# Decoder step on one core: the convolution's group norm moved between the third pair's values, its four reciprocals made one, output scales folded into the splits, the last cached values in two more slots

## The reference

```python
x = post(x, 0.5 * swiglu_1(mod(x, 0)), 0)
q, k, v, glu = project(mod(x, 1), w_in)
attn = moba(q, k, v)             # samples: 2048 cached keys/values each, 8 heads of 64
y = depthwise_conv(glu) + b_dw   # 31 taps, 512 channels
g = y.reshape(..., 8, 64)        # 8 groups of 64 channels
g = (g - mean(g)) * rsqrt(mean((g - mean(g)) ** 2) + 1e-5)
conv = silu(g.reshape(y.shape) * gn_g + gn_b)
m = concat([attn * beta_attn, conv * beta_conv]) @ w_out
x = post(x, m, 1)
x = post(x, 0.5 * swiglu_2(mod(x, 2)), 2)
```

## Time and profile before

| what | value |
|---|---|
| median of 3 runs | 952.88 us (950.6 to 952.88) |
| profiled execution: its time | 953.04 us |
| its span, first to last instruction | 951.2 us |
| mean granted TensorE clock | 0.957 |
| TensorE busy | 865.2 us, 91% |
| VectorE, ScalarE, GpSimd busy | 51%, 36%, 28% |

### The profile page before, as it was taken

One profiled execution on the slowest core, in us unless ns is written; L12 is line 12 of the kernel. 1 busy time (PEld: TensorE's weight loads), 2 busy tenths in 40 slices (PEclk: granted clock), 3 DMA queues, 4 the chain that ended last, 5 costly groups with the idle time before them and its releaser, 6 DMA issues.

```text
span 951.2 us, 16893 instructions
## 1 busy us (share of the span) xinstructions
PE 865.2 (91%) x6704; PEld 759.1 (80%) x6704; DVE 481.5 (51%) x764; ACT 342.7 (36%) x466; POOL 266.0 (28%) x319
## 2 busy tenths in 40 slices
PE   6699999997899988999987889867989999999997
PEld 3499989996799968988664556437879999999995
DVE  1543433431333387753686776564774434444436
ACT  2323332331222254455442324253463333342223
POOL 2020000000010014999999999300320000000000
PEclk9599999999899998999999989888999999999999
DMA  9958777777577434334897999994415454644401
GB/s 301 347 184 262 232 221 258 246 233 259 190 236 231 144 110 133 128 94 162 264 359 264 350 359 370 348 348 137 133 46 177 140 166 137 183 143 145 133 1 56
DMA packets 181521, 195.78 MB, mean 206 GB/s; under 512 B 11811, under 2 KB 163609, under 8 KB 181445
## 3 DMA queue, kind: packets, MB, share of 16 engines
q1 hardware_dynamic: 174541, 188.38, 61.3%
q10 hardware_dynamic: 6624, 6.33, 2.1%
q0 software_dynamic: 288, 0.14, 0.1%
HBM read 192.01 MB, written 3.17 MB: 205 GB/s over the span
## 4 chain that ended last, share of the span: by engine, by line
PE 76%; DVE 13%; DMA 4%; ACT 3%; issue 2%; SPq 1%; ACTq 0%; DVEq 0%
PE bank L1389 19%; PE bank L1390 18%; PE bank L1391 18%; PE bank L1605 5%; PE bank L1365 3%; PE bank L1630 3%; DVE wlo L956 2%; DVE kT L1194 2%; PE bank L1402 1%; PE bank L1700 1%; PE bank L1403 1%; PE bank L1404 1%; PE bank L1354 1%; DMA xrow<-in_x_sample 1%; DMA raw<-in_ffn_wg 1%
## 5 line engine op out<-in xcount | busy, mean ns | idle before, releaser
L956 DVE TENSOR_TENSOR wlo<-raw,whi 128x2048 fp32r<-128x2048 f32 (+1 forms) x80 | 190.8, 2386 | 264.1 <-ACT whi L649 264.1
L1389 PE MATMUL bank<-mh,whi 128*128 128x320 f32 x824 | 262.1, 318 | 4.5 <-DVE wlo L956 4.5
L1390 PE MATMUL bank<-ml,whi 128*128 128x320 f32 x824 | 256.5, 311 | 0.0
L1391 PE MATMUL bank<-mh,wlo 128*128 128x320 f32 x824 | 256.4, 311 | 0.0
L649 ACT CAST whi<-raw 128x2048 fp32r<-128x2048 f32 (+1 forms) x80 | 148.6, 1863 | 258.3 <-PE bank L1391 171.3
L1389 PEld LDWEIGHTS bank<-mh,whi 128*128 128x128 f32 x824 | 156.8, 190 | 15.3 <-issue 10.3
L1390 PEld LDWEIGHTS bank<-ml,whi 128*128 128x128 f32 x824 | 156.9, 190 | 0.0
L1391 PEld LDWEIGHTS bank<-mh,wlo 128*128 128x128 f32 x824 | 156.6, 190 | 0.0
L1389 PE MATMUL bank<-hh,whi 128*128 128x320 f32 x352 | 109.7, 312 | 0.0
L1390 PE MATMUL bank<-hl,whi 128*128 128x320 f32 x352 | 108.6, 309 | 0.0
L1391 PE MATMUL bank<-hh,wlo 128*128 128x320 f32 x352 | 108.6, 308 | 0.0
(11 more groups left out here) (233 smaller groups left out, 1161.2 us busy)
## 6 DMA issues: line engine op xcount, KB each, us to landing
araw<-in_w_ada SPq DMA_DIRECT2D x28, 1024.0 KB, 5.1
raw<-in_ffn_wg SPq DMA_DIRECT2D x22, 1024.0 KB, 7.5
raw<-in_ffn_wu SPq DMA_DIRECT2D x22, 1024.0 KB, 6.9
raw<-in_cache_v SPq DMA_DIRECT2D x68, 256.0 KB, 6.1
raw<-in_ffn_wd SPq DMA_DIRECT2D x16, 1024.0 KB, 6.5
raw<-in_cache_k SPq DMA_DIRECT2D x64, 256.0 KB, 4.2
raw<-in_w_in SPq DMA_DIRECT2D x10, 1024.0 KB, 5.4
raw<-in_w_ada SPq DMA_DIRECT2D x8, 1024.0 KB, 12.3
```

The source lines that it names most:

```text
L956: dve.tensor_tensor(wl(slot_w(phase, u))[:, 0:size], landed(phase, u)[:, 0:size], wh(slot_w(phase, u))[:, 0:size].bitcast(F32), ALU.subtra ...
L1389: pe.matmul(bank[:, b, 0:T], wh(slot)[:, c], h_, start=(start and n == 0), stop=False)
L1390: pe.matmul(bank[:, b, 0:T], wh(slot)[:, c], l_, start=False, stop=False)
L1391: ins = pe.matmul(bank[:, b, 0:T], wl(slot)[:, c], h_, start=False, stop=(stop and n == len(parts) - 1))
```

## The change

- `group_means` is hooked after step 3 of `pair_values(2)`, the subtractions stand between two steps of the pair 3 softmax, the squares after its exponentials, and `group_variances` between `pair_values(2)` and `pair_probs(3)`.
- The variances of the 8 groups are taken with a 128 x 32 matrix into 32 partitions for each chunk, all in bank 0. So one root and one reciprocal of 128 x 320 stand for four of each, and `group_scales`, after step 2 of `pair_values(3)`, spreads the result back to 128 partitions by four matmuls over 32 rows.
- ScalarE writes `mh` as value times output scale, and VectorE writes `ml` as value times scale less `mh`. The separate scaling falls away.
- `hi(WOUT, 0)` comes before the Silu, `hi(WOUT, 1)` after the convolution's splits; `lo(WOUT, 0)` before the convolution's `ml`, `lo(WOUT, 1)` after.
- The last eight value chunks go to slots 0, 1, 2, 3, 6, 7, 2, 3. Chunks 60 and 61 lie in `kvw` and no longer wait for steps 0 and 1 of pair 3; `lo` of `WOUT` 0 and 1 wait until they are consumed.
- `conv_half(1)` is cut in two, with `attn_turn(3)` between the halves.
- The constants grow by 160 columns, and `acc` lies in an old tile.

```diff
 def kv_slot(kvi):
-    return kvi % (KV_RING if kvi < KVN - 8 else RING)
+    return kvi % KV_RING if kvi < KVN - 8 else (0, 1, 2, 3, 6, 7, 2, 3)[kvi - KVN + 8]
...
             for u in range(2, WOUT[2]):
-                load(WOUT, u, cols(i["w_out"], slice(UC * u, UC * u + UC)), NCH * UC, (v_used, 24 + 3 + u))
+                load(WOUT, u, cols(i["w_out"], slice(UC * u, UC * u + UC)), NCH * UC, (v_used, 24 + u - 1))
...
+            def group_squares():
+                act.wait_ge(stored_conv, 16 * DB)
+                for c in range(NCC):
+                    act.wait_ge(gc_ready, c + 1)
+                    act.activation(tmp[:, c, :], yT[:, NCC + c, :], ACT.Square).then_inc(gq_ready, 1)
...
                 probs(j)
+                if j == 3:
+                    group_squares()
                 acc_out(j - 1)
...
+            act.wait_ge(gv_mm, 1)
+            act.activation(tmp[:, 0, :], bank[:, 0, 0:T], ACT.Sqrt, bias=con[:, C_EPS:C_EPS + 1]).then_inc(gs_ready, 1)
+            hi(WOUT, 0)
+            act.wait_ge(ge_mm, NCC)
             for c in range(NCC):
                 act.wait_ge(gx_ready, c + 1)
                 act.activation(tmp[:, c, :], yT[:, NCC + c, :], ACT.Silu, scale=par2[:, 4 + c:5 + c], bias=par2[:, 8 + c:9 + c]).then_inc(gy_ready, 1)
+                act.wait_ge(gy_ready, c + 1)
+                act.mul(mh[:, NCC + c, :], tmp[:, c, :], par2[:, 16 + c:17 + c]).then_inc(mh_ready, 1)
+            hi(WOUT, 1)
+            acc_out(3)
+            attn_out(3)
+            act.wait_ge(av_evac, 4)
+            act.wait_ge(pv_out, 4)
+            for c in range(NHP):
+                act.mul(mh[:, c, :], yT[:, c, :], par2[:, 12 + c:13 + c]).then_inc(mh_ready, 1)
...
                 if phase is WOUT and u < 2:
-                    dve.wait_ge(v_used, 24)
+                    dve.wait_ge(v_used, 24 + 5 + u)
...
                 bias_ready(j)
+                if j == 3:
+                    for c in range(NCC):
+                        dve.wait_ge(gm_mm, c + 1)
+                        y = yT[:, NCC + c, :]
+                        dve.tensor_tensor(y, y, bank[:, c, 0:T], ALU.subtract).then_inc(gc_ready, 1)
                 sums_ready(j)
...
+            dve.wait_ge(gs_ready, 1)
+            dve.reciprocal(tmp[:, 1, :], tmp[:, 0, :]).then_inc(gr_ready, 1)
             for c in range(NCC):
+                dve.wait_ge(ge_mm, c + 1)
                 y = yT[:, NCC + c, :]
+                dve.tensor_tensor(y, y, bank[:, c, 0:T], ALU.mult).then_inc(gx_ready, 1)
+            def low_mix(n, src, at):
+                c = MIX_ORDER[n]
+                dve.wait_ge(mh_ready, 16 + n + 1)
+                dve.scalar_tensor_tensor(ml[:, c, :], src, par2[:, at:at + 1], mh[:, c, :].bitcast(F32), ALU.mult, ALU.subtract).then_inc(ml_ready, 1)
+            lo(WOUT, 0)
             for c in range(NCC):
+                low_mix(c, tmp[:, c, :], 16 + c)
             lo(WOUT, 1)
             for c in range(NHP):
+                low_mix(NCC + c, yT[:, c, :], 12 + c)
...
+                steps = {0: lambda: gate_sum(j), 2: lambda: max_swap(j), 5: lambda: prob_sum(j)}
+                if j == 3:
+                    steps[3] = group_means
+                pair_values(j - 1, steps)
+                if j == 3:
+                    group_variances()
                 pair_probs(j)
                 attn_turn(j - 1)
...
             def group_variances():
                 for c in range(NCC):
                     pe.wait_ge(gq_ready, c + 1)
-                    pe.matmul(bank[:, c, 0:T], gnones, tmp[:, c, :], start=True, stop=True).then_inc(gv_mm, 1)
+                    ins = pe.matmul(bank[QG * c:QG * c + QG, 0, 0:T], con[:, C_GSUM:C_GSUM + QG], tmp[:, c, :], start=True, stop=True)
+                ins.then_inc(gv_mm, 1)
+
+            def group_scales():
+                pe.wait_ge(gr_ready, 1)
+                for c in range(NCC):
+                    pe.matmul(bank[:, c, 0:T], con[QG * c:QG * c + QG, C_GOUT:C_GOUT + P], tmp[QG * c:QG * c + QG, 1, :],
+                              start=True, stop=True).then_inc(ge_mm, 1)
...
-            pair_values(3, {0: group_means, 2: group_variances, 6: lambda: conv_half(0)})
-            conv_half(1)
+            pair_values(3, {2: group_scales, 6: lambda: conv_half(0, 0, NCC)})
+            conv_half(1, 0, 2)
             attn_turn(3)
+            conv_half(1, 2, NCC)
```

More of the change, by code:

```diff
@@ L66 @@
 C_TURN = C_SWAP + P
-C_N = C_TURN + P
+C_GSUM = C_TURN + P
+C_GOUT = C_GSUM + QG
+C_N = C_GOUT + P
 def constants():
@@ L104, in constants @@
             c[:, at:at + QG] = ((h[:, None] == 2 * (col[None, :QG] // 8) + e) & (r[:, None] == r_) & (t[:, None] == col[None, :QG] % 8))
+    c[:, C_GSUM:C_GSUM + 2] = (p[:, None] // 64 == np.arange(2)[None, :]) / 64.0
+    c[:, C_GOUT:C_GOUT + P] = p[:, None] % QG == col[None, :] // 64
     return c
@@ L282, in build @@
             qo = sb("qo", [P, DB, NHP, QG], F32, scope)
-            acc = sb("acc", [P, 2, 2 * P], F32, scope)
             vtok = sb("vtok", [P, 2, AW], F32, scope)
@@ L301, in build @@
             pr = sb("pr", [P, 3, 2], F32, scope)
+        acc = ps_[:, 0:2, 0:2 * P]
         s_two = (s_even[:, 0:PAST + 2 * NS].rearrange("p (b c) -> p b c", b=2), s_odd[:, :, :])
@@ L1738, in next_pair @@
                     pe.wait_ge(pt_evac, 5 * j)
-                pair_values(j - 1, {0: lambda: gate_sum(j), 2: lambda: max_swap(j), 5: lambda: prob_sum(j)})
+                steps = {0: lambda: gate_sum(j), 2: lambda: max_swap(j), 5: lambda: prob_sum(j)}
[4 more added lines that the diff above has]
+                    group_variances()
                 pair_probs(j)
                 attn_turn(j - 1)
-            for j in range(1, 4):
-                next_pair(j)
-            pe.wait_ge(pt_evac, 20)
             def group_means():
@@ L1758, in group_variances, with conv_half @@
                     pe.wait_ge(gq_ready, c + 1)
-                    pe.matmul(bank[:, c, 0:T], gnones, tmp[:, c, :], start=True, stop=True).then_inc(gv_mm, 1)
+                    ins = pe.matmul(bank[QG * c:QG * c + QG, 0, 0:T], con[:, C_GSUM:C_GSUM + QG], tmp[:, c, :], start=True, stop=True)
[5 more added lines that the diff above has]
+                              start=True, stop=True).then_inc(ge_mm, 1)
+            for j in range(1, 4):
+                next_pair(j)
+            pe.wait_ge(pt_evac, 20)
             first = [(2 * u + cc, slot_w(WOUT, u), cc, (n_ready, w_used)[cc]) for u in range(2) for cc in range(2)]
-            def conv_half(u):
+            def conv_half(u, c0, c1):
                 pe.wait_ge(w_lo, WOUT[0] + u + 1)
-                products(first[2 * u:2 * u + 2], m_parts(MIX_ORDER[:NCC]), lambda n: pe.wait_ge(ml_ready, 16 + n + 1), stop=False)
-            pair_values(3, {0: group_means, 2: group_variances, 6: lambda: conv_half(0)})
-            conv_half(1)
+                products(first[2 * u:2 * u + 2], m_parts(MIX_ORDER[c0:c1]), lambda n: pe.wait_ge(ml_ready, 16 + c0 + n + 1),
+                         start=c0 == 0, stop=False)
+            pair_values(3, {2: group_scales, 6: lambda: conv_half(0, 0, NCC)})
+            conv_half(1, 0, 2)
             attn_turn(3)
+            conv_half(1, 2, NCC)
             products(first, m_parts(MIX_ORDER[NCC:]), lambda n: pe.wait_ge(ml_ready, 16 + NCC + n + 1), start=False)
```

22 lines of the change are left out of this document (2 added, 20 removed).

## The result

The changed kernel took 941.95 us (median of 4, 938.21 to 943.44), the kernel before 951.74 us (median of 4). The ratio is 0.9892, with a 95% interval of 0.9867 to 0.9917: some 10.3 us faster, 7.9 to 12.7. With more rounds it came out at 0.9905 (0.9884 to 0.9927), 9.0 us. The forecast was a gain of 8.9 us and a time of 944.1, between 941.5 and 947.8. The gain was about right.

What follows compares the result with a forecast made beforehand. The norm's chain was taken to hold `conv_half(0)` through `wlo`, with DMA data as second limit. Gains of 5.7, 1.4 and 1.8, in all 8.9 us, from 953.04 gave 944.1, range 941.5 to 947.8.

Steps and rivals of the forecast that it cites:

- What bounded the kernel: Before `conv_half(0)`: 5.65 us idle for `wlo`, held by the norm's chain; behind it, DMA data set value step 6.
- The front part: Norm work moved to pair 2: means 2.35 us, variances 0.3 us; pair 3's values start at 623.75 instead of 621.1.
- The middle: From the root to the last `ml` in pair 3: `conv_half(0)` has its operands 3.0 us before step 6 ends.
- rival of a late chain by table loads: Silu and `mul` share no table, seven more loads cost 9.0 us, gain 5.6; chance 0.12, at 946.5 to 950.
- Transfers: Loads of the last value chunks: chunks 60 to 62 land when they did; the slots' change counts 0.
- The end: From `conv_half(0)` to the attention's first matmul: gains of 5.7, 1.4 and 1.8 us, in all 8.9.
- the three terms: `conv_half(0)` starts 5.7 us earlier, runs 1.4 shorter, and step 7 to the attention's first matmul takes 1.8 less.
- Against the profiled execution's 953.04 ... 944.1: Whole kernel: the gain of 8.9 us set against the one profiled execution of 953.04 gives 944.1.
- step 6 cannot start before 637.8: Pair 3's value step 6: its start is set by DMA data, a chunk every 3.0 us, whatever the norm does.
- the likeliest case: Whole kernel: time of 944.1, chance 0.80, own range 941.5 to 946.5.

Runs made afterwards that it cites:

- again: The kernel before, unchanged, run against itself and profiled a second time: ratio 0.9985 (0.9968 to 1.0001).

## Why the prediction was right, and where it was off

**What bounded the kernel.** Right. The wait for `wlo` before `conv_half(0)` was the chain of the norm, and behind it stood the data of the last values. The run with a megabyte less shows the second limit, the run with six more reciprocals brings the first one back.

**The front part.** Right that it costs nothing that counts, with its sizes off. The subtractions and the squares fitted in the idle times named. From step 3 of pair 2 to pair 3's values it took 12.43 us (606.69 to 619.12; 12.44 in the second profile), before 11.71 at a clock partly down (0.81 from 606 to 624) and 11.03 in the second profile at the full one. So the moved work costs 0.7 or, both at the full clock, 1.4 us, and the forecast had 2.65. That pair 3's values started at 619.12, not 623.75, has another reason for the larger part: step 3 of pair 2 had already started 2.7 us earlier (606.69 for 609.38), ahead of the change. The page "TensorEngine Tiling (Array Packing)" of the Trainium skill, in "Tiling Modes", has four tiles for matrices of 32 rows as for 32 columns, working side by side; the trace agrees. `group_scales` took 0.82 us, against 2.42 for four full-width matmuls of the same 320 columns, and the forecast had taken the upper bound of 2.35.

**The middle.** Right that it arrives in time: 3.0 us of reserve forecast, 1.9 found, since step 4 ran in part at half clock (1.70 us) and `wlo` waited for it, and since the four `ml` then took 1.93 us, for 1.5. The scaled writes on ScalarE were not the pace: the last ended at 631.64, for 636.1. That is because `group_scales` was done at 623.9, for 630.2, and `WOUT` 0 had landed by 623.77, for 625.7. The rival of a late chain by table loads did not come: two loads, and Silu alternates with the scaled write without one. The further drain that the Trainium skill counts in "ScalarE: Activation LUTs", "What ACT_TABLE_LOAD costs", does not show here: the load ends at 620.32 and the root starts at 620.33, and the same holds at 626.97 and 626.99. Nor does it show ahead of the load, which starts 0.02 us after the work before it ends (619.02 and 625.67). So 1.28 us is the price in this place.

**Transfers.** Right, as far as the runs can tell: with the slots undone the time stays within its interval, and chunk 60 is used when it was although it was issued 0.8 us later.

**The end.** In the first pair of profiles the three terms came out as 5.7, 1.6 and 1.7 for 5.7, 1.4 and 1.8. Only the third is confirmed by more than one pair. The first two fit so well by luck, since forecast and check both used the one execution whose norm came late. Over three profiles with the old norm (before, again, and with the cut alone) step 6 to `conv_half(0)` took 7.58, 6.08 and 6.14 us and `conv_half(0)` 6.49, 5.69 and 5.93. Over five with the new one it was 1.87 each, within 0.01, and 4.91, 4.88, 5.67, 4.78 and 4.95. By the means the terms are 4.7, 1.0 and 1.7, in all 7.4 and not 8.9. What lies between 7.4 and the 9.0 measured (6.9 to 11.0) is not located. In the first changed profile the clock rose after 2.6 us of `conv_half(0)`, 4.4 after the start of step 6; the forecast had 5.2.

**The step that failed** is the last one, "Against the profiled execution's 953.04 ... 944.1", with the range built on it. It takes one execution for the base, and it puts the stretch up to step 6 at nothing, by "step 6 cannot start before 637.8". That holds for that one execution. Step 6 started at 637.80, 637.16, 635.50 and 639.84 in the four profiles with the norm at its old place, and at 635.78, 636.51, 636.61, 637.38, 635.26 and 636.74 in six with it at the new place and the whole stream (634.49 in a seventh, with the idle matmuls). What these follow is the moment at which SyncE comes to chunk 56, between 601.3 and 606.5 and before the change acts; the 33.0 to 33.9 us from there are the same in both kernels. So the 2.0 us by which the changed profile was ahead of the sum are scatter: 1.5 of them lie before the change, and 0.5 are less than the width of those distances. What makes SyncE come to chunk 56 early or late stays open.

The profile used was in two respects a slow one: its time was 1.3 us above the median that the kernel before then showed, 951.74, and it came late to pair 3, in part by a stretch at half clock, so that the wait before `conv_half(0)` was 5.65 and not 4.14 as in the second profile. With 8.9 taken from 951.74 the forecast would have been 942.8. The median of three shown beforehand, 952.88, would not have helped; medians of 11 to 23 executions later were 950.35 to 951.19. The range gave the likeliest case 1 us each way for scatter, while executions of the kernel before spread over 946.1 to 952.9 in one session; its lower edge, 941.5, left nothing for a median from a few runs. So of the gain a part was right by luck, and of the time the base was wrong.

The forecast also didn't say that merging and moving are alternatives. It read the 5.7 us as won by both. The move gets all of it without the merge; the merge without the move takes 4.2 us off the chain, which was just enough in a run whose data were late.

## What to carry to other kernels

Where two limits stand one behind the other, the gain of removing the first is what lies between them, and any one of several edits may get all of it: try each alone before keeping both. Then look at the waits of the second limit as room. Here the convolution's matmuls fitted between the arrivals of the last values, and only then was it worth keeping TensorE's clock up. And do not take the size of a wait, or the base of a time, from one profile: it may hold a slow stretch of its own. Here the wait was 4.1 to 5.7 us in three profiles of code that is the same up to there, and the base moved by more than 2 us between medians, so the spread between executions is the least width of a range. When two profiles differ ahead of a change, look for the first point at which they do.

## What the runs showed of the hardware that had not been expected

- Matmuls on 32 rows overlap as those on 32 columns do: four float32 matmuls of 320 columns took 0.82 us on 32 x 128 tiles, 0.75 on 128 x 32, and 2.42 on the full array.
- Six idle matmuls (3.50 us) in one wait were worth nothing when two waits of 1.9 us followed (0.9904 against 0.9905), and some 2 us when these were filled (0.9857 against 0.9880, with overlapping intervals).
- Issuing a chunk 0.8 us later did not move its use (630.64 against 630.55) while the DMA engines were full (share 1.08 to 1.10 and 345 to 348 GB/s from 606 to 640).
